# All three products of an expert in one go, in a two-layer mixture-of-experts stage

## The reference, cut to what matters

```python
def run(args):
    tok, wt, e = args
    xb = h_pad[tok]                                          # 64 tokens x 1024
    hid = jax.nn.silu(xb @ w_gate[e]) * (xb @ w_up[e])       # 1024 -> 512
    return (hid @ w_down[e]) * wt[:, None]                   # 512 -> 1024
```

## Time and profile before

| | |
|---|---|
| runs | 2702.43, 2703.35, 2688.87 us; median 2702.43 |
| the profiled execution | 2701.66 us, its span 2699.8 us |
| granted TensorE clock, mean of the span | 0.856 |
| TensorE matmul busy | 2320.5 us (86%), 8503 instructions |
| VectorE, ScalarE, GpSimd busy | 800.2 us (30%), 405.4 us (15%), 282.2 us (10%) |
| weight loads from high-bandwidth memory | 592.94 MB on the queue of SP |
| gate and up products, L966 and L969 | 1040 matmuls each, mean 679 and 680 ns |
| down products, L984 | 1040 matmuls, mean 601 ns |

### The profile page before, as it was taken

How to read it: one execution, slowest core, us unless ns; L and a number is a source line. 1 busy time by engine, 2 the same in 40 slices (tenths; PEclk the granted TensorE clock), 3 DMA queues, 4 the chain that set the end, 5 groups by cost and what they waited for, 6 DMA issues and landing times.

```text
span 2699.8 us, 22654 instructions
## 1 busy us (share of the span) xinstructions
PE 2320.5 (86%) x8503; PEld 1244.7 (46%) x8503; DVE 800.2 (30%) x1665; ACT 405.4 (15%) x837; POOL 282.2 (10%) x293
## 2 busy tenths in 40 slices
PE   7989999999999989988688888887499688888885
PEld 3466755446565544654533333333256333333331
DVE  1122367415166631962411111110343311111111
ACT  2122000114100021651200000000222100000000
POOL 0000000000000000850011111110000111111110
PEclk9966999995999999559699998898686799999997
DMA  9721367741337921001199999997620289999994
GB/s 249 257 99 46 140 230 274 261 151 55 117 129 260 383 105 63 32 16 49 68 366 382 384 388 386 396 392 315 249 109 8 91 348 397 395 395 390 395 398 188
DMA packets 128145, 631.42 MB, mean 234 GB/s; under 512 B 14359, under 2 KB 16567, under 8 KB 102225
## 3 DMA queue, kind: packets, MB, share of 16 engines
q1 hardware_dynamic: 109056, 592.94, 55.8%
q0 software_dynamic: 17840, 34.33, 4.8%
q10 hardware_dynamic: 1184, 3.35, 0.3%
HBM read 625.47 MB, written 26.57 MB: 242 GB/s over the span
## 4 chain that ended last, share of the span: by engine, by line
PE 25%; DMA 21%; DVE 3%; issue 2%; SPq 1%; ACT 1%; POOLq 0%; POOL 0%; DVEq 0%; ACTq 0%
DMA ring<-ex_up 20%; PE PS L966 12%; PE PS L984 5%; PE PS L957 2%; PE PS L417 2%; PE PS L683 1%; PE PS L532 1%; PE PS L550 1%; SPq L1545 1%; PE PS L540 1%; DMA arena<-tokens_d,arena 1%; DMA arena<-rows_d 1%; PE PS L969 0%; PE PS L324 0%; DVE arena L1278 0%
## 5 line engine op out<-in xcount | busy, mean ns | idle before, releaser
L966 PE MATMUL PS<-ring,arena 128*64 128x512 f32 x1040 | 539.9, 679 | 147.7 <-DMA ring<-ex_up 145.2
L969 PE MATMUL PS<-ring,arena 128*64 128x512 f32 x1040 | 540.3, 680 | 0.0
L966 PEld LDWEIGHTS PS<-ring,arena 128*64 128x64 f32 x1040 | 156.0, 156 | 467.6 <-issue 454.2
L417 PE MATMUL PS<-ring,arena 128*128 128x512 f32 (+1 forms) x736 | 300.9, 565 | 6.5 <-DVE arena L370 3.3
L1247 DVE COPY arena<-PS 128x512 f32<-128x512 f32 x64 | 44.3, 692 | 717.5 <-PE PS L957 717.5
L724 PE MATMUL PS<-arena,ring 128*128 128x256 f32 x1024 | 234.3, 392 | 18.2 <-DMA ring<-ffn_w 15.5
L984 PE MATMUL PS<-ring,arena 128*64 128x512 f32 x1040 | 238.9, 601 | 1.5 <-DVE arena L1243 1.5
L724 PEld LDWEIGHTS PS<-arena,ring 128*128 128x128 f32 x1024 | 200.6, 197 | 57.1 <-issue 26.9
L735 PE MATMUL PS<-ring,arena 128*128 128x512 f32 x512 | 222.7, 593 | 0.3 <-DMA ring<-ffn_w 0.3
L417 PEld LDWEIGHTS PS<-ring,arena 128*128 128x128 f32 x736 | 139.2, 193 | 147.4 <-issue 135.8
L532 PE MATMUL PS<-arena 64*128 64x256 f32 (+2 forms) x256 | 145.8, 697 | 12.9 <-DVE arena L600 6.4
(11 more groups left out here) (226 smaller groups left out, 2038.0 us busy)
## 6 DMA issues: line engine op xcount, KB each, us to landing
ring<-ex_gate SPq DMA_DIRECT2D x65, 2048.0 KB, 14.4
ring<-ex_up SPq DMA_DIRECT2D x65, 2048.0 KB, 18.6
ring<-ex_down SPq DMA_DIRECT2D x65, 2048.0 KB, 9.8
ring<-ffn_w SPq DMA_DIRECT2D x32, 2048.0 KB, 11.1
ring<-mod_w SPq DMA_DIRECT2D x24, 2048.0 KB, 13.8
ring<-a_w_qkv SPq DMA_DIRECT2D x9, 2048.0 KB, 40.8
ring<-b_w_qkv SPq DMA_DIRECT2D x6, 2048.0 KB, 15.3
ring<-w_in_ab SPq DMA_DIRECT2D x3, 2048.0 KB, 18.3
```

What stands on the lines that cost most here:

```text
L417: mm = pe.matmul(PS[:, u % 4, 0:w.width], q.src[:, k, w.t * P:(w.t + 1) * P], w8(w.tile, w.width)[:, k, :], start=(k == 0), stop=(k == KD ...
L966: g = pe.matmul(PS[0:CAP, u, :], xT[:, k, :], w8(gate)[:, k, :], start=(k == 0), stop=(k == KD - 1))
L969: h = pe.matmul(PS[CAP:P, u, :], xT[:, k, :], w8(up)[:, k, :], start=(k == 0), stop=(k == KD - 1))
```

## The change

The pipelining by one expert is given up. On TensorE an expert now runs `inner(e)`, `tokens_in(e+1)`, `hidden_turned(e)`, `outer(e)`; ScalarE runs `gate_out(e)`, `rows_out(e)`; VectorE `tokens_out(e+1)`, `hidden_out(e)`. The helper functions, buffers, loads, gathers and scatters are the same, and so are the number and the sizes of all instructions. The overflow part is not touched.

```diff
@@ TensorE
+            last = NE // 2 - 1
             tokens_in(0, 0)
-            inner(0, 0, 0)
-            tokens_in(1, 0)
-            hidden_turned(0)
-            with pe.Fori(0, NE // 2 - 1) as i:
-                e = 2 * i + 1
-                inner(e, 1, i)
-                tokens_in(0, i + 1)
-                outer(e - 1, 0, i)
-                hidden_turned(e)
-                inner(e + 1, 0, i + 1)
-                tokens_in(1, i + 1)
-                outer(e, 1, i)
-                hidden_turned(e + 1)
-            last = NE // 2 - 1
+            with pe.Fori(0, last) as i:
+                for u in range(2):
+                    inner(2 * i + u, u, i)
+                    tokens_in(1 - u, i + u)
+                    hidden_turned(2 * i + u)
+                    outer(2 * i + u, u, i)
+            inner(NE - 2, 0, last)
+            tokens_in(1, last)
+            hidden_turned(NE - 2)
+            outer(NE - 2, 0, last)
             inner(NE - 1, 1, last)
-            outer(NE - 2, 0, last)
             hidden_turned(NE - 1)
             outer(NE - 1, 1, last)
@@ ScalarE
-            gate_out(0, 0)
-            gate_out(1, 0)
-            rows_out(0, 0)
-            gate_out(0, 1)
-            rows_out(1, 0)
-            with act.Fori(1, NE // 2 - 1) as i:
-                gate_out(1, i)
-                rows_out(0, i)
-                gate_out(0, i + 1)
-                rows_out(1, i)
-            last = NE // 2 - 1
-            gate_out(1, last)
-            rows_out(0, last)
-            rows_out(1, last)
+            for u in range(2):
+                gate_out(u, 0)
+                rows_out(u, 0)
+            with act.Fori(1, NE // 2) as i:
+                for u in range(2):
+                    gate_out(u, i)
+                    rows_out(u, i)
@@ VectorE
             tokens_out(0, 0)
-            tokens_out(1, 1)
-            hidden_out(0, 0, 0)
             with dve.Fori(0, NE // 2 - 1) as i:
-                tokens_out(2 * i + 2, 0)
-                hidden_out(2 * i + 1, 1, i)
-                tokens_out(2 * i + 3, 1)
-                hidden_out(2 * i + 2, 0, i + 1)
-            hidden_out(NE - 1, 1, NE // 2 - 1)
+                for u in range(2):
+                    tokens_out(2 * i + u + 1, 1 - u)
+                    hidden_out(2 * i + u, u, i)
+            tokens_out(NE - 1, 1)
+            for u in range(2):
+                hidden_out(NE - 2 + u, u, NE // 2 - 1)
```

## The result

The changed kernel took 2727.59 us (median of three runs, 2720.89 to 2727.63) against 2702.43 before; the ratio is 1.0099 with a 95% interval of 1.0058 to 1.0141. The prediction was 2722. The profiled execution took 2720.89 us; its span is 2719.1 us against 2699.8, so the two traces differ by 19.3 us.

What follows compares the result with a forecast made beforehand. The kernel before was bound by a loop of expert transfers and TensorE through buffer slots; after, TensorE would be the limit at 16.74 us an expert. Stages +2.8 and +16.8, together +19.6 on 2702.4, gave 2722 us; range 2675 to 2765.

Steps and rivals of the forecast that it cites:

- The loop through the slots: Expert loads: in-order queue stands at the down slot, delaying gate and up; earlier release gives back at most 23.8 and 24.0 us.
- The four outstanding tiles: Loading queue: four tiles outstanding instead of three when a gate/up starts because its up tile has just landed.
- TensorE's cycle at full clock: TensorE, per expert: 7.02 + 2.95 + 1.53 + 3.59 = 15.09 us, under the transfer bounds of 16.2 and 15.6.
- The clock, 1.65 us an expert: TensorE in both expert stages: half clock after idle pieces costs 1.65 us an expert, making the cycle 16.74 us.
- no alternation: Sign of being right: gate/up starts 16.5 to 17.1 us apart in both stages alike, without alternating.
- a clock of about 0.5 at their head: Sign of being right: down products near 5 us, with a granted clock of about 0.5 at their start.
- the mean of the three places: Mean clock loss, 1.43 us, over three old-trace places with dense work, 1.51 us idle, small turn; the forecast leaned above it.
- The sum: Whole kernel: stage one +2.8 us and stage two +16.8, together +19.6 on the median 2702.4, giving 2722.
- The held clock: First rival, chance 0.15: TensorE's clock holds between gate/up and down product, transfers decide; -55 us, 2647.
- Break-even: Both expert stages: time unchanged at a clock loss of 1.34 us an expert, over 64 experts.
- The long fall in every expert: Third rival, chance 0.05: clock loss of 2.77 us in every expert; +92 us, 2794.
- The DMA share: Sign of being right: DMA share near 0.93 in the first stage, with loads issued as soon as gate/up ends.

Runs made afterwards that it cites:

- e2_half_loads: Kernel after, each weight load of the 32 experts bringing only the first half of its tile; 2727.22 us in one execution.
- e5_fill_fit: Kernel after with unused dense matmuls cut to fit TensorE's two idle pieces (512 and 256 columns, then 256); 2641.53 us, ratio 0.9792.
- e4: Kernel after with two steps swapped on TensorE and VectorE: hidden rows turned first, next tokens after them; 2645.10 us, ratio 0.9807.
- e1_fill: Kernel after with four unused dense matmuls of 512 columns in TensorE's two idle pieces, three and one; 2699.58 us, ratio 1.0008.
- e3_gates_first: Kernel before with only the loading queue edited: gate and up of expert e+1 issued ahead of down of expert e; 2650.67 us, ratio 0.9838.

## Why the prediction was right, point by point

**The loop through the slots, and where the change would move it.** Right. Gate and up are issued at the end of gate/up, the wait for ex_up went from 58.6 us to nothing in the stretch shown, and TensorE is what is late next. e2_half_loads shows that the last is true and not only plausible. The four outstanding tiles, which the prediction gave for a gate/up that starts because its up tile has just landed, didn't occur here: gate/up waits for no tile, and at 1593.04 only the next up, issued at 1583.31, is under way, with down following at 1593.25.

**TensorE's cycle at full clock, 15.09 us.** Right as a sum of parts: 6.97 to turning the tokens, 2.95, 1.53 and, were the clock full, 3.6. One expert of stage one kept its clock (gate/up at 1442.85 and the next at 1457.78) and needed 14.93; most of the difference is in the overlap of the last step with the next gate/up. In stage two no expert kept it, but e5_fill_fit gives 15.10 to 15.14 there.

**The clock, 1.65 us an expert.** Right in mechanism and sign, too small in size. Gate/up starts came 16.63 and 17.3 to 17.5 us apart in stage one, often by turns, and 16.8 and 17.4 to 17.5 in stage two; the mean without the slow first one was (1866.08 - 1357.44) / 30 = 16.95 in stage one and (2674.79 - 2163.07) / 30 = 17.06 in stage two, where 16.74 was forecast and 16.5 to 17.1 given as the sign. The means are inside that, but "no alternation" was wrong. The mis-sized term is the loss in each expert: 16.95 - 14.93 = 2.02 us in stage one and 17.06 - 15.12 = 1.94 in stage two, against 1.65. A slow down product takes 5.35 us in most experts and 5.84 to 6.14 in many others, those in which the clock had fallen before it began. I had taken 1.53 from the overflow block, whose last part ran at full clock (granted 1.00 from 1903.70 to 1905.60), with one long fall in ten. The sign "a clock of about 0.5 at their head" held only in part: in the product at 1604.49 the head ran at 1.00 and the fall came 1 us later. That the clock would fall in practically every expert, as the 1.65 assumed against the mean of the three places, was right: 63 of 64. In stage two the wait before the down product was also 0.70 us instead of 0.52 in many experts (20.9 us over 30 experts, against 15.5 in stage one), which no step of mine had; it is in the 15.12.

```profile
2292.61 1.01 PE L975 MATMUL PS<-const,arena 64*128 64x64 f32 x5 [1.51 <-DVE arena L1229]
...
2294.25 1.02 POOL L1295 DMA_INDIRECT rows_d<-arena  x1 [1.42 <-issue]
2294.32 5.35 PE L984 MATMUL PS<-ring,arena 128*64 128x512 f32 x16 [0.70 <-DVE arena L1232]
```

What makes it 0.70 was not tested.

**The sum.** Its total was nearly exact, 19.6 forecast against 19.3 between the traces (and 25.2 between the medians), but by two errors that cancel. The stages were given +2.8 and +16.8; they cost +8.8 and +25.6, together 34.4. The longer cycle accounts for the 14.8 us in between: 30 x 0.21 + 30 x 0.32 = 15.9, less about 1 us at the two ends of the stages. Against that stand 15.0 us outside the stages that I hadn't looked for at all. 6.8 of them are at the end of stage one. There the gather for the overflow block shared the DMA engines before with the block's weight loads (6 MB, issued from 1868.82 to 1869.72); after, the loads are issued at about the same time (1867.17 to 1868.08), the experts end 8 us later, the loads are nearly through, and the gather is quick. From the two chains in order of time, before and after:

```profile
1875.71 9.53 DMA arena<-tokens_d,arena
```

```profile
1883.74 2.78 DMA arena<-tokens_d,arena
```

So that lateness cost almost nothing. A further 2.5 us are the overflow block, where the clock was better after: its gate/up took 1 us less, and its down product 3.65 us against 5.14 in rows 6. 5.0 us lie between the overflow block and stage two, in instructions that neither kernel changes. The granted clock is behind them as well: its mean there was 0.69 before (244.7 us) and 0.71 after (239.6), and the same 32 matmuls of L417 took 17.00 us at 1948.67 before and 15.58 at 1947.27 after. That part took 244.7 and 244.8 us in the kernel before and in e4, the two in which the down product of the overflow block was slow (5.14 and 5.18 us), and 239.2 to 240.2 in the seven others. What the clock there depends on was not tested; no step of the change aims at it, so this gain was luck, and so were the 0.7 us ahead of stage one.

**The rivals.** The held clock was priced at 2647, 55 us under the kernel before; e5_fill_fit, which is just that case made real, took 2641.5, 56 us under it. The mechanism of this rival and its price were right, its condition was not met. Break-even was put at a loss of 1.34 us: e1_fill, with a cycle of 16.60 (1.5 over 15.09), broke even within 0.1%; its two stages took 532.3 and 532.1 us, 10.5 together over the kernel before, and the gains outside the stages made up for that. The long fall in every expert did not occur; gate/up ran at full clock (mean 592 ns between 1420 and 1800 us).

The Trainium skill (TensorE: Matmul & The Clock Gate, section on HAM oscillation), read as the prediction read it, would have the clock fall only behind a long gap. Here it fell in nearly every expert around idle pieces of 1.51 and 0.52 us with small turns between them, and dense work in those pieces held it; the measurement decides.

**The DMA share.** Wrong as a sign: 0.93 was given for stage one, 0.95 measured over the whole of it and 0.99 from 1420 to 1800 us. I had worked it out as bytes over time (0.96 x 16.2 / 16.74). In this kernel the share stood near 1 in a stretch in which a load was always under way, while the rate was 390 GB/s, against 407 in e3_gates_first at 1.01. So the two shares hide a difference in rate; what lowers the rate was not tested.

## What to carry to other kernels

A wait on one engine that hides behind another step costs nothing to uncover only as long as the engine's whole cycle, at the clock that it will then be granted, stays under the next limit; so price the cycle at both clocks, and look for a place in the old trace where the new order already occurs, such as a first expert or an overflow path. When an in-order queue holds slots back, reorder that queue first: one edit in the loading order gave 47 us here (2650.7 against 2697.7), without any change on TensorE. A filler takes away idle time and adds dense work at once, so by itself it doesn't tell which of the two holds the clock. And test what limits by taking bytes away, not by the busy share of the DMA engines.

## What the runs showed that I had not expected

- Filling 1.51 and 0.52 us of idle TensorE time with unused dense matmuls made the kernel about 3% faster than the same kernel without them (ratio 0.9792 against 1.0099, both against the kernel before beside them; 2641.5 and 2727.6 us).
- Halving the expert loads changed the time by under 1 us (one execution), at a DMA share of 0.58 instead of 0.99.
- Turning the next tokens after the hidden rows instead of before them halved the number of slow down products (31 instead of 63) and was worth 2.9% in ratio (0.9807 against 1.0099).
- A float32 matmul of 512 columns with all 128 rows and columns takes 0.86 us at full clock and stands in the trace as two records 0.43 us apart (e1_fill).
- In the trace shown the clock fell 1 us after the dense work had begun again, not in the idle pieces before it.
